# Seven block products in another order, sums of h split 3:1 between two engines, and gate products inside two attention ends

## Reference, cut to what matters

```python
def _mixer(h, w_in, ...):          # sliding-window attention (swa), conv, fox, dsa attention
    ...
    ys = jnp.stack([y_a, y_d, y_f, y_s], axis=2)
    proj = jnp.einsum('blnc,ncd->blnd', ys, w_branch)
    gates = jax.nn.sigmoid(g.reshape(bsz, L, N_BRANCH, D_MODEL))    # g: columns of h @ w_in
    return jnp.sum(gates * proj, axis=2) @ w_o

def reference(x, c, ...):
    ...
    x = x + g1 * _rmsnorm(_mixer(h, ...), norm_g[l, 1])
    h = _rmsnorm(x, norm_g[l, 2]) * (1.0 + sc2) + sh2
    y = (jax.nn.silu(h @ w_gate[l]) * (h @ w_up[l])) @ w_down[l]
    return x + g2 * _rmsnorm(y, norm_g[l, 3])
```

## Time and profile before

| | |
|---|---|
| median of three runs | 1792.37 us (1791.25 to 1794.73) |
| the profiled execution | 1790.29 us, span 1788.5 us |
| granted clock of PE, mean | 0.984 |
| busy PE | 1683.7 us, 94% |
| busy DVE, ACT, Pool | 58%, 34%, 47% |

### The profile page before, as it was taken

The page is one execution under the profiler, slowest core; times in us unless marked ns, Lnnn a source line. Parts: engine busy times, 40 slices in busy tenths (PEclk is TensorE's granted clock), DMA queues, the critical chain, the costliest instruction groups (busy, mean ns, idle before and its releaser), DMA issues.

```text
span 1788.5 us, 22702 instructions
## 1 busy us (share of the span) xinstructions
PE 1683.7 (94%) x8036; PEld 1403.0 (78%) x8036; DVE 1041.2 (58%) x1732; ACT 609.8 (34%) x1067; POOL 838.0 (47%) x542
## 2 busy tenths in 40 slices
PE   2899999998999999989999999899999999999996
PEld 2887878787888888878788788677887877888785
DVE  5614745568999999467475336643444254334428
ACT  2433335373332222256334444223222222322223
POOL 0621130103446566510587224966557556655654
PEclk9999999998999999999999999999999999999998
DMA  8121141010111111420873501111012011111214
GB/s 300 68 61 58 59 112 34 15 51 30 44 44 59 44 44 48 160 42 1 306 251 122 208 36 36 42 64 65 30 47 70 28 57 56 61 33 47 70 44 181
DMA packets 37452, 139.88 MB, mean 78 GB/s; under 512 B 4624, under 2 KB 4624, under 8 KB 37392
## 3 DMA queue, kind: packets, MB, share of 16 engines
q1 hardware_dynamic: 35152, 131.75, 21.5%
q0 software_dynamic: 2240, 7.34, 1.9%
HBM read 118.62 MB, written 14.16 MB: 74 GB/s over the span
## 4 chain that ended last, share of the span: by engine, by line
PE 87%; DVE 7%; DMA 2%; ACT 1%; issue 1%; SPq 0%; POOL 0%; DVEq 0%; ACTq 0%
PE ps L607 25%; PE ps L608 25%; PE ps L609 25%; PE ps L806 4%; PE ps L785 2%; DVE y_t L2162 2%; PE ps L711 1%; DMA region_b<-in_w_ada 1%; PE ps L712 1%; DVE region_a L2115 1%; PE ps L637 1%; DMA raw<-in_w_ffn 1%; DVE region_a L2183 0%; PE ps L629 0%; PE ps L817 0%
## 5 line engine op out<-in xcount | busy, mean ns | idle before, releaser
L607 PE MATMUL ps<-h_t,w_t 128*128 128x512 f32 x1112 | 437.2, 393 | 2.3 <-DVE y_t L1905 1.4
L608 PE MATMUL ps<-h_t,w_t 128*128 128x512 f32 x1112 | 434.4, 391 | 0.0
L609 PE MATMUL ps<-h_t,w_t 128*128 128x512 f32 x1112 | 434.2, 390 | 0.0
L607 PEld LDWEIGHTS ps<-h_t,w_t 128*128 128x128 f32 x1112 | 209.8, 189 | 47.5 <-issue 4.1
L608 PEld LDWEIGHTS ps<-h_t,w_t 128*128 128x128 f32 x1112 | 209.9, 189 | 43.7 <-issue 0.7
L609 PEld LDWEIGHTS ps<-h_t,w_t 128*128 128x128 f32 x1112 | 209.7, 189 | 43.9
L1452 POOL TENSOR_TENSOR w_t<-raw,w_t 128x1280 fp32r<-128x1280 f32 (+1 forms) x50 | 140.6, 2812 | 205.4 <-ACT w_t L1060 115.3
L2130 DVE TENSOR_TENSOR y_f<-ps,y_f 128x512 f32<-128x512 f32 x100 | 69.0, 690 | 255.8 <-PE ps L609 255.0
L1593 POOL TENSOR_TENSOR w_t<-raw,w_t 128x512 fp32r<-128x512 f32 x80 | 108.2, 1358 | 151.6 <-ACT w_t L1343 150.8
L1797 DVE MAX8 top<-region_b 128x8 f32<-128x384 f32 (+5 forms) x192 | 157.9, 882 | 17.3 <-issue 16.7
L1800 DVE MATCH_REPLACE8 region_b<-top,region_b 128x384 f32<-128x384 f32 (+5 forms) x192 | 166.1, 876 | 0.0
(11 more groups left out here) (271 smaller groups left out, 3331.5 us busy)
## 6 DMA issues: line engine op xcount, KB each, us to landing
region_b<-in_w_ada SPq DMA_DIRECT2D x48, 512.0 KB, 4.5
raw<-in_w_ffn SPq DMA_DIRECT2D x46, 512.0 KB, 3.8
raw<-in_w_gates SPq DMA_DIRECT2D x32, 640.0 KB, 3.9
region_d<-in_w_ffn SPq DMA_DIRECT2D x20, 512.0 KB, 3.8
raw<-in_w_z SPq DMA_DIRECT2D x18, 512.0 KB, 3.3
region_a<-in_x SPq DMA_DIRECT2D x8, 512.0 KB, 11.3
mix_dram<-region_a SPq DMA_DIRECT2D x8, 512.0 KB, 5.9
region_a<-mix_dram SPq DMA_DIRECT2D x8, 512.0 KB, 6.5
```

The lines of the kernel that those rows point to most:

```text
L607: pe.matmul(o, a_hi, m_hi, start=first, stop=False, skip_group_check=more)
L608: pe.matmul(o, a_hi, m_lo, start=False, stop=False, skip_group_check=more)
L609: return pe.matmul(o, a_lo, m_hi, start=False, stop=last, skip_group_check=more)
```

## The change

STEP_BANK and step_moving put the seven products in another order: b11, T2, T4, T3, T1, b21, b22 becomes b11, T2, b21, T3, T4, T1, b22, and the last product begins a bank anew. So quarter (0, 0) is complete after the third step of seven, and quarter (0, 1) ("upper") gets one more add: bank 3 after the sixth step and bank 1 after the seventh. DVE's order in a group has twelve adds instead of ten, and the product and rest of (0, 0) come first. ACT's order of splits and silu follows. T3 and T1 change places: T3 and T2 lie in wide_b, T1 over b12.

The sums T3, T2, T4 and T1 are split over their four k parts of 512 columns: three to DVE, one to Pool, each with its own rests, where before T1, T2 and T4 were DVE's in two parts each and T3 half and half. T1, the last, is cut up between DVE's evacuations `first_out`.

In the last two units of both attentions PE's 48 matmuls of the first gate tile's product with h are put in eight pieces of six between turns, values and turn_out, into banks 4 and 5 (`gate_beside`); the product with y follows behind (`gate_first`). SP's last reload of z no longer waits for the end of the second attention: parts 1 to 7 wait one by one for units inside it, and part 0 is neither written nor read back, since the keys of the second attention move from places 0 and 1 to 1 and 2.

```diff
-STEP_BANK = (0, 1, 2, 1, 3, 0, 3)
-STEP_NEW = (True, True, True, False, True, False, False)
+STEP_BANK = (0, 1, 0, 1, 2, 3, 1)
+STEP_NEW = (True, True, False, False, True, True, True)
...
-        dsa_keys = (stack_a[:, 0], stack_a[:, 0]), (stack_a[:, 1], stack_a[:, 1])
+        dsa_keys = (stack_a[:, 1], stack_a[:, 1]), (stack_a[:, 2], stack_a[:, 2])
...
-        t1, t2 = (wide_b[:, 0], wide_b[:, 1]), (wide_b[:, 2], wide_b[:, 3])
-        t1_f, t2_f = (wide_f[:, 0], wide_f[:, 1]), (wide_f[:, 2], wide_f[:, 3])
-        t3, t3_f = b12, tuple(h_f[:, a, 0:4, HALF:L] for a in range(2))
+        t3, t2 = (wide_b[:, 0], wide_b[:, 1]), (wide_b[:, 2], wide_b[:, 3])
+        t3_f, t2_f = (wide_f[:, 0], wide_f[:, 1]), (wide_f[:, 2], wide_f[:, 3])
+        t1, t1_f = b12, tuple(h_f[:, a, 0:4, HALF:L] for a in range(2))
         t4, t4_f = (tuple(y[:, 1, a].rearrange("p b (c n) -> p (b c) n", c=2) for a in range(2)) for y in (y_t, y_f))
-        step_moving = (b11, t2, t4, t3, t1, b21, b22)
+        step_moving = (b11, t2, b21, t3, t4, t1, b22)
+        t_of, t_f_of = {1: t1, 2: t2, 3: t3, 4: t4}, {1: t1_f, 2: t2_f, 3: t3_f, 4: t4_f}
+        t_part = [slice(0, 3), slice(3, 4)]
...
-        LATE = ((1, 0), (1, 1), (0, 0), (0, 1))
+        LATE = ((0, 0), (1, 0), (1, 1), (0, 1))
...
-            src = raw_at[b if s in (2, 4) else a]
-            return src[:, HALF:L] if s in (2, 5, 6) else src[:, 0:HALF]
+            src = raw_at[b if s in (4, 5) else a]
+            return src[:, HALF:L] if s in (2, 4, 6) else src[:, 0:HALF]
...
-            sp.wait_ge(s_spill, 16 * KT)
-            for dt in range(KT):
...
+            after = U_DSA + HEADS * TT
+            for dt, (s, n) in enumerate(((s_logit, after), (s_logit, after), (s_lg, after), (s_t, after - 1), (s_t, after),
+                                         (s_pv, after - 1), (s_pv, after)), 1):
+                sp.wait_ge(s, n)
+                sp.dma_start(z[:, dt], mix_dram[:, dt, :]).then_inc(s_refill[dt >= 4], 16)
...
-            def attention(u0, n):
+            def attention(u0, n, gate=None):
+                beside = gate_beside(gate)
...
                     turn(u)
+                    if u >= end - 2:
+                        next(beside)
                     if u - 2 >= u0:
                         turn_out(u - 2)
                     if u > u0:
                         values(u - 1)
+                    if u >= end - 2:
+                        next(beside)
                 turn_out(end - 2)
                 values(end - 1)
+                next(beside)
                 turn_out(end - 1)
+                for _ in beside:
+                    pass
+
+            def gate_beside(T):
+
+                if T is None:
+                    for _ in range(5):
+                        yield
+                    return
+                pe.wait_ge(s_w_lo, T + 1)
+                for half in range(2):
+                    for k in range(KT):
+                        c, w = slice(half * HALF, (half + 1) * HALF), slice(k * P, (k + 1) * P)
+                        product(ps[:, 4 + half, :], w_t[:, T % 2, 0, w], w_t[:, T % 2, 1, w], h_hi[:, k, c],
+                                h_lo[:, k, c], k == 0, k == KT - 1)
+                        if k % 2:
...
+                for half in range(2):
+                    tile_half(ps[:, 2 + half, :], T % 2, half, KT, BT, y_hi(buf), y_lo(buf)).then_inc(s_z, 1)
...
-            gate_pairs(T_AFS, 0)
+            gate_first(T_AFS, 0)
+            gate_tile(T_AFS + 1, 0)
+            gate_pairs(T_AFS + 2, 0, KT // 2 - 1)
...
+                if g == 0 and STEP_NEW[s] and s < 6:
                     pe.wait_ge(s_yf, count(i, 2 * TT, 2 * TT + STEP_BANK[s] - 3))
+                if s == 2:
+                    pe.wait_ge(s_first, count(i, 2, g + 1))
                 if s == 3:
-                    pe.wait_ge(s_u, count(i, 10, 5 * g + 1))
-                if s == 5:
-                    pe.wait_ge(s_first, count(i, 2, g + 1))
+                    pe.wait_ge(s_u, count(i, 12, 6 * g + 1))
                 if s == 6:
-                    pe.wait_ge(s_u, count(i, 10, 5 * g + 4))
-                if s in (1, 2, 3, 4):
-                    T = (2, 4, 3, 1)[s - 1]
-                    pe.wait_ge(s_t_lo[T], 2 if T == 3 else 1)
...
+                if s in (1, 3, 4, 5):
+                    pe.wait_ge(s_t_lo[{1: 2, 3: 3, 4: 4, 5: 1}[s]], 2)
                 m_hi, m_lo = step_moving[s]
                 hi, lo, new = slot_hi[n % SLOTS], slot_lo[n % SLOTS], STEP_NEW[s]
...
+                split_hi(T0 + 1, n=GT)
+                gate_tile(T0, m0, bank=4)
+                split_hi(T0 + 2, n=GT)
+                gate_tile(T0 + 1, m0 + 2)
+                gate_pairs(T0 + 2, m0 + 4, n - 1)
...
-                    act.wait_ge(s_step, count(i, STEPS, 6))
+                    act.wait_ge(s_step, count(i, STEPS, 3))
...
-                    act.wait_ge(s_u, count(i, 10, {0: 3, 1: 4, 3: 5}[v]))
+                    act.wait_ge(s_u, count(i, 12, {1: 3, 2: 4, 3: 6}[v]))
...
-                for n in (6, 7, 8, 9):
+                slot_split(i, 6)
+                slot_split(i, 7)
+                silu(i, 0)
+                for n in (8, 9, 10):
                     slot_split(i, n)
-                silu(i, 0)
-                slot_split(i, 10)
                 silu(i, 1)
+                slot_split(i, 11)
                 silu(i, 2)
-                slot_split(i, 11)
                 slot_split(i, 12)
+                first_term(i, 1)
                 silu(i, 3)
-                first_term(i, 1)
-                for n in (13, 14, 15, 16):
+                for n in (13, 14, 15):
                     slot_split(i, n)
                 a_hi(i, 0)
+                slot_split(i, 16)
                 slot_split(i, 17)
                 a_hi(i, 1)
...
+            def t_hi(T, who):
+                act.wait_ge(s_t_sum[T][who], 1)
+                k = t_part[who]
+                act.activation(t_of[T][0][:, k], t_f_of[T][1][:, k], ACT.Copy).then_inc(s_t_hi[T], 1)
...
+            first_silu(0)
+            first_a_hi(0)
+            t_hi_all(3)
+            first_silu(1)
+            t_hi_all(2)
+            first_a_hi(1)
+            t_hi_all(4)
+            first_silu(2)
+            first_a_hi(2)
             for n in range(14, 18):
                 first_down_split(n)
-            t_hi(2, s_t2_sum)
             first_silu(3)
-            t_hi(1, s_t1_sum)
             first_a_hi(3)
-            t_hi(4, s_t4_sum)
             slot_split(1, 0)
-            t_hi(3, s_t3_sum[0], slice(0, 2))
             slot_split(1, 1)
-            t_hi(3, s_t3_sum[1], slice(2, 4))
+            t_hi_all(1)
             for n in range(2, SLOTS):
                 slot_split(1, n)
...
+            for j in range(2):
+                split_lo(T_GD + j + 1, n=GT)
+                if j == 1:
+                    pool.wait_ge(s_refill[0], 48)
+                gate_tile(T_GD + j, j, False)
+            pool.wait_ge(s_refill[1], 64)
+            with order.loop(KT // 2 - 2, 4) as i:
+                for j in range(2):
+                    split_lo(T_GD + 2 + j + 1, i, 2, GT)
+                    gate_tile(T_GD + 2 + j, 2 + j, False, i)
...
-                    pool.wait_ge(s_slot_lo, made(i, n0 + 5, ahead))
+                    pool.wait_ge(s_slot_lo, made(i, n0 + 2, ahead))
...
+            def t_sum(T):
+
+                o_hi, o_lo = hi_lo(t_f_of[T])
+                if T in (1, 3):
+                    (p_hi, p_lo), (q_hi, q_lo) = (hi_lo(a) for a in ((b12_f, b11_f) if T == 1 else (b22_f, b12_f)))
+                    order.mark(pool.tensor_tensor(o_lo, p_lo, q_lo, ALU.subtract))
+                    order.then_wait(pool.tensor_tensor(o_hi, p_hi, q_hi, ALU.subtract))
+                    other = o_hi
+                elif T == 2:
+                    pool.wait_ge(s_t_sum[3][1], 1)
+                    (p_hi, other), before = hi_lo(b11_f), hi_lo(t3_f)[1]
+                    order.then_wait(pool.tensor_tensor(o_lo, before, p_hi, ALU.add))
...
+                pool.tensor_tensor(o_lo, o_lo, other, ALU.add).then_inc(s_t_sum[T][1], 1)
...
+            def t_rest(T):
+                pool.wait_ge(s_t_hi[T], 2)
+                if T in (2, 3):
+                    pool.wait_ge(s_t_sum[{3: 2, 2: 4}[T]][1], 1)
+                hi, lo = hi_lo(t_of[T])
+                pool.tensor_tensor(lo, hi_lo(t_f_of[T])[1], hi.bitcast(F32), ALU.subtract).then_inc(s_t_lo[T], 1)
...
+            t_sum(3)
+            t_sum(2)
+            first_a_lo(0)
+            t_sum(4)
+            first_a_lo(1)
+            for T in (3, 2, 4):
+                t_rest(T)
+            first_a_lo(2)
...
             first_a_lo(3)
             pool.wait_ge(s_z, 2 * T_FFN + 8)
+            t_sum(1)
             slot_rest(1, 0)
             for n in (1, 2, 3):
                 combine(1, 0, n)
             slot_rest(1, 1)
+            t_rest(1)
...
+            dve.wait_ge(s_h, 4 * TT)
+            dve.wait_ge(s_x1_out, 16 * TT)
```

(44 more changed lines are left out.)

158 lines of the change are left out of this document (65 added, 93 removed).

## The result

| | before | changed |
|---|---|---|
| median, 20 runs each | 1792.09 us (1788.58 to 1797.40) | 1796.28 us (1792.12 to 1802.30) |
| ratio | | 1.0021 (1.0012 to 1.0030) |
| profiled execution, span | 1790.29, 1788.5 | 1796.66, 1794.8 |
| mean granted clock | 0.984 | 0.983 |

The change is slower by 0.21%, 3.8 us (2.2 to 5.4). The forecast was +7.8: the sign is right, the time lies in the range, the size is twice what came.

A forecast was written before the change was run, and what follows sets the result against it. PE, busy 94% of the span, bounds the kernel. Terms 6.3 + 0.7 + 6.8 - 2.3 + 0 - 3.7 = +7.8 us gave 1800.2 us after allowing for the runs' median; range 1786 to 1808.

The forecast's parts named there:

- 1.3 of the emptied half: Both attention ends: gate tile 2 waits 1.3 us until ScalarE, table load included, has emptied half 0 of tile 1.
- no change there: Start of feed-forward part: the half-clock stretch of 6.8 us behind the first down product's wait stays as before.
- Who excludes whom: DVE and Pool instructions with two SBUF operands exclude each other; a DVE subtract against busy Pool costs 1.7 us, not 0.69.
- Part 1: Order of the seven products: nine group waits +6.3 us (-1.8 to +14), last group +0.7, clock falls +6.8.
- All nine have 2.3 to 2.5: Hand-overs to down products: PE waits 2.3 to 2.5 us in all nine groups, taken as 2.45, +6.3 us in all.
- Part 2: Sums of h split 3:1 between DVE and Pool: new wait about 3.8 us for 6.5 before, -2.3 us (-6.5 to 0).
- Both waits are long enough for a half-clock stretch like the one of 6.8 us: Start of feed-forward part: old and new wait each bring a half-clock stretch like that of 6.8 us; nothing gained.
- the 0.4 behind T1: Start of feed-forward part: a later PE wait of 0.4 us behind the sum T1, beside the new 3.8.
- Parts 3 and 4: Gate pieces in the attention ends: first end 0 us (-3.5 to +2), second end -3.7 us (-5 to 0).
- go earlier, not later: SP's queue at the second attention end: loads behind z's reloads are issued earlier; counted as nothing, bound +-1 us.
- B: Rival: the hand-over tail doesn't grow if the combination's weights land later; 1780 to 1787 us, faster, chance 0.15.
- D: Rival: gate pieces fill nothing at both attention ends and all nine groups fall; +15 us, 1807, slower, chance 0.10.

The follow-up runs named there:

- the cut rest: Changed kernel with Pool's rest of the convolution's output (2048 columns) cut in four instructions of 512 columns; 1786.72 us, ratio 0.9983 to before.

## Why the prediction was right and wrong

The direction and the mechanism at the hand-overs were right. The size was not. The step that failed is the "1.3 of the emptied half", put on both attention ends: that wait never came. A second step, "no change there" for the clock behind the first down product, failed in the same direction. Both are worked out below.

**Who excludes whom: right.** The tail that the prediction wrote out is the tail of five hand-overs, 2.35 for 2.5, and holding Pool back took 1.5% off the changed kernel, 27 us by the two ratios. The Trainium skill (SBUF — State Buffer, "SBUF: two separate sides") calls the port pair that the two engines share an exclusive lock; the runs agree, down to an addition of four columns: 4.12 us behind a long Pool instruction, 0.89 behind a short one.

**Part 1: right in kind.** "All nine have 2.3 to 2.5" holds for 13 of 18 in two traces, if 2.65 and 2.73 of the first group are let in; the other five have 3.41 to 3.44, which the prediction had as a bound only (and that bound, 9 x 3.4 - 15.7, is 14.9, not 14). Waits +9 for +6.3, last group 0.65 for 0.7, seven falls for seven. In the trace the groups cost 15.8 for 13.8. Timed beside the other parts, the order costs 9.3: there the old order has lost some of its short waits too (18.3 us on average in three traces, for 15.2 in four of the kernel before). So the parts are not additive: some 3 us of waits and a fall or two that the sum books under the order come with the other parts without it.

**Part 2: the wait right, the clock not.** The 3.8 us are there to 0.1, and their cause too (L1749 is the weight rest). The closeness has some luck in it: the prediction's own working gives 1123.7 - 1120.1 = 3.6, and the 0.4 behind T1 did not come. But the step "Both waits are long enough for a half-clock stretch like the one of 6.8 us, no change there" failed: the stretch was 3.4 us, a gain of 1.5 more. Measured -3.7 in the trace for -2.3. Across the traces the length goes with the wait, though not strictly: behind the 6.3 us of the old sums it was 6.8 us in all six, behind the 3.8 it was 3.4 in five of eight, 6.8 in two, and none in one.

**Parts 3 and 4: one term wrong in both.** The new wait of 1.3 us for the emptied half never came. It was made mostly of the table load, 1.28, behind PE's last matmul. In the changed kernel the first gate tile stands outside the loop, and the row shown for the first attention end has the load at 416.63, right behind ScalarE's last weight copy and long before PE is through (ScalarE then idles 15.66 us; at the second end 2.63). Only the sigmoid is left, and PE has no wait behind it. The rest of the terms held at the first end: wait 3.45 for 3.5, and a fall. It gave -2.05 for a forecast of 0, -1.3 with the term taken out. The rest lies in the count of before: the prediction had 7.6 us above PE's work there. By the traces with the cut rest (23.4, of it 0.2 a wait) it was 8.6, and 6.6 in the changed kernel for a forecast 6.3. The second end gave -5.2, which with the term taken out is the forecast -5.0. The two terms of 1.3 and the stretch of part 2 are 4.1 us of the forecast 7.8.

**Part 4, what was counted at nothing.** For the loads queued behind z's reloads the prediction counted nothing, since they "go earlier, not later". In five of the twelve profiled executions with the pieces at the second end PE waits 2.0 to 2.7 us at the third gate tile, in none of the six without. The second end takes 62.1 to 63.8 us in those five, 59.2 to 60.2 in the other seven, and 64.4 to 65.2 without the pieces. ACT and PE of the kernel with the cut rest:

```profile
865.55 1.27 ACT L1093 ACTIVATE w_t<-raw 128x1280 fp32r<-128x1280 f32 x1 [7.11 <-DMA raw<-in_w_gates]
```

```profile
870.97 0.79 PE L608 MATMUL ps<-h_t,w_t 128*128 128x512 f32 x1 [2.44 <-POOL w_t L1501]
```

The five differ from the seven in how long the load of these weights takes: 6.8 to 7.5 us from issue to landing, against 4.8 to 5.5 (5.56 in before). Four loads for the modulation are issued right ahead of it in all of them, and in before too, so their order does not tell the two cases apart. Why it lands late in five stays open. The trace of the changed kernel is one of the seven, so nothing of this is in its 6.3 us.

**The sum.** In the traces the changed places come to -2.05 - 5.2 - 3.7 + 15.8 = +4.9 us for a forecast of 7.8: 5.0 less at the ends and the sums, 2.0 more in the groups. So one error hid a part of the other. The pair of profiled executions differs by 6.3, since 1.5 more comes from places that the change does not touch; that is taken as chance, since at the two largest of them (up to 304, and 377.9 to 403.0) the four traces of before differ by 1.3 and 1.2 us among themselves. The medians give 3.8 to 4.2, and what is left between 4.9 and these can't be told apart: executions of one kernel on one chip spread over 9 to 14 us, and the timed ones leave no trace. Of the rivals, B (the tail doesn't grow) and D (the pieces fill nothing) are out. C's time, 1793.4, is nearer to the measured one than the forecast's (2.9 us off against 3.9), but its reason is wrong, since the clock did fall oftener.

## What to carry to other kernels

Before an instruction is added to or moved on DVE, look at what GpSimd runs at that time. With GpSimd out of the way the new order waits 0.73 us per group where the old one mostly waits nothing; with GpSimd beside it PE waits 2.35 or 3.41, 1.0 more per group than before (0.2 to 2.3), and the clock falls in seven groups instead of three. Where both engines meet in a short stretch on the critical path, hold GpSimd back with one wait if its work has slack (here one line gave 1.1% in the kernel before and 1.5% in the changed one), or cut its instruction in pieces (0.38%). And where a wait has two values across executions, find the event that decides and its margin before counting on the mean. Last, before a difference between two traces is booked on a change, cut the stretch down to the place that the change touches.

## What the runs showed that was not expected

- How thin the edge is: of two hand-overs whose combinations begin 0.67 and 0.68 us after the start of PE's last matmul, one waits 2.22 us and one 1.12.
- The table load of ScalarE is placed with the code: at the first gate tile of a loop it stood behind the wait for PE (14.35 us idle before it), in straight code ahead of it (416.63, and 854.96 at the second end).
- A fall of the clock followed 2.35 us of wait in some hand-overs and not in others: of the eighteen in two traces of the changed kernel fourteen had one.
